# A fourth split weight block behind the inner norms, the silu table behind the root, and the last input chunk product by product, in a two-layer hybrid decoder

## What is computed

```
for l in range(DEPTH):
    ada = silu(c) @ w_ada[l] + b_ada[l]
    sh1, sc1, g1, sh2, sc2, g2 = split(ada, 6)
    u = x * (1 + sc1) + sh1
    mix = token_mixer(u, w_in[l], ...)
    x = layer_norm(ALPHA * x + (1 + g1) * mix, ln1_g[l], ln1_b[l])
    u = x * (1 + sc2) + sh2
    a, b = split(u @ w_ffn_in[l], 2)
    x = layer_norm(ALPHA * x + (1 + g2) * ((silu(a) * b) @ w_ffn_out[l]), ln2_g[l], ln2_b[l])
```

## Time and profile before

| what | value |
|---|---|
| time, median of 3 | 1686.99 us (1684.29 to 1687.72) |
| the profiled execution: its time, its span | 1685.16 us, 1683.3 us |
| instructions | 21326 |
| PE busy | 1623.5 us (96%) |
| DVE busy | 1001.8 us (60%) |
| ACT busy | 623.5 us (37%) |
| mean granted TensorE clock | 0.991 |
| DMA | 193.07 MB, mean 115 GB/s |

### The profile page before, as it was taken

One profiled execution on the slowest core, in us unless ns is written; L12 is line 12 of the kernel. 1 busy time (PEld: TensorE's weight loads), 2 busy tenths in 40 slices (PEclk: granted clock), 3 DMA queues, 4 the chain that ended last, 5 costly groups with the idle time before them and its releaser, 6 DMA issues.

```text
span 1683.3 us, 21326 instructions
## 1 busy us (share of the span) xinstructions
PE 1623.5 (96%) x8406; PEld 1277.1 (76%) x8406; DVE 1001.8 (60%) x1557; ACT 623.5 (37%) x1117; POOL 51.7 (3%) x102
## 2 busy tenths in 40 slices
PE   6999999999999999999989999999999999999997
PEld 3778677677778888888868776766777788888886
DVE  2777687758685555546567657766557533333444
ACT  3432454445253322222253325445534533222221
POOL 1000000000001001100000000000000000000000
PEclk8999999999999999999999999999999999999999
DMA  9754222134327666664427231111222233333332
GB/s 304 219 168 128 74 63 64 51 99 140 101 64 211 187 194 183 188 185 148 140 53 200 75 88 38 39 38 34 80 88 88 84 92 100 101 100 119 91 93 74
DMA packets 278450, 193.07 MB, mean 115 GB/s; under 512 B 8344, under 2 KB 264912, under 8 KB 278352
## 3 DMA queue, kind: packets, MB, share of 16 engines
q1 hardware_dynamic: 264112, 147.95, 30.4%
q0 software_dynamic: 12320, 43.11, 8.6%
q10 hardware_dynamic: 1920, 0.66, 0.2%
HBM read 189.59 MB, written 2.10 MB: 114 GB/s over the span
## 4 chain that ended last, share of the span: by engine, by line
PE 87%; DVE 7%; ACT 2%; issue 2%; DMA 1%; SPq 0%; DVEq 0%; ACTq 0%
PE banks L1587 22%; PE banks L1589 22%; PE banks L1588 22%; PE banks L1709 3%; PE banks L1740 3%; PE banks L1768 2%; DMA ada_first<-in_w_ada_dram 1%; PE banks L1629 1%; PE banks L1715 1%; PE banks L1625 1%; PE banks L1626 1%; DVE w_lo L957 1%; PE banks L1719 1%; PE banks L1644 1%; PE banks L1645 1%
## 5 line engine op out<-in xcount | busy, mean ns | idle before, releaser
L1587 PE MATMUL banks<-u_hi,w_hi 128*128 128x512 f32 x1144 | 470.5, 411 | 15.8 <-DVE w_lo L957 12.5
L957 DVE TENSOR_TENSOR w_lo<-ring,w_hi 128x1024 fp32r<-128x1024 f32 (+2 forms) x243 | 290.6, 1198 | 298.9 <-ACT w_hi L696 298.0
L1589 PE MATMUL banks<-u_hi,w_lo 128*128 128x512 f32 x1144 | 449.5, 393 | 0.0
L1588 PE MATMUL banks<-u_lo,w_hi 128*128 128x512 f32 x1144 | 449.0, 392 | 0.0
L696 ACT ACTIVATE w_hi<-ring 128x1024 fp32r<-128x1024 f32 (+2 forms) x246 | 253.8, 1032 | 198.5 <-PE banks L1589 74.5
L1587 PEld LDWEIGHTS banks<-u_hi,w_hi 128*128 128x128 f32 x1144 | 216.5, 189 | 67.9 <-DVE w_lo L957 13.2
L1589 PEld LDWEIGHTS banks<-u_hi,w_lo 128*128 128x128 f32 x1144 | 216.2, 189 | 46.5
L1588 PEld LDWEIGHTS banks<-u_lo,w_hi 128*128 128x128 f32 x1144 | 217.2, 190 | 35.8
L849 ACT ACTIVATE probs<-banks,neg_max 128x128 f32<-128x128 f32 (+3 forms) x192 | 99.2, 525 | 159.5 <-DVE neg_max L1376 159.5
L1587 PE MATMUL banks<-h_hi,w_hi 128*128 128x512 f32 x352 | 138.5, 394 | 0.0
L1589 PE MATMUL banks<-h_hi,w_lo 128*128 128x512 f32 x352 | 137.0, 389 | 0.0
(11 more groups left out here) (253 smaller groups left out, 2145.4 us busy)
## 6 DMA issues: line engine op xcount, KB each, us to landing
ring<-in_w_ffn_in_dram SPq DMA_DIRECT2D x88, 512.0 KB, 3.9
ada_ring<-in_w_ada_dram POOLq DMA_DIRECT2D x80, 512.0 KB, 4.3
ring<-in_w_in_dram SPq DMA_DIRECT2D x72, 512.0 KB, 3.8
ring<-in_w_ffn_out_dram SPq DMA_DIRECT2D x32, 448.0 KB, 3.4
ada_first<-in_w_ada_dram SPq DMA_DIRECT2D x16, 512.0 KB, 8.5
ring<-in_w_out_dram SPq DMA_DIRECT2D x16, 512.0 KB, 3.6
ring<-in_w_ffn_out_dram SPq DMA_DIRECT2D x16, 512.0 KB, 4.1
w<-in_cmp_w_k_dram SPq DMA_DIRECT2D x8, 512.0 KB, 5.6
```

The lines of the kernel that those rows point to most:

```text
L957: V.tensor_tensor(lo, src, hi.bitcast(fp32), ALU.subtract).then_inc(split_lo, 1)
L1587: M(bank, wh[:, block], sh[:, k, :], start=start, stop=False)
L1588: M(bank, wh[:, block], sl[:, k, :], start=False, stop=False)
L1589: return M(bank, wl[:, block], sh[:, k, :], start=False, stop=stop)
```

## The change

1. fb1 in both layers and kwn in layer 1 (FOURTH_SPLIT, `is_fourth`) get a split buffer of their own, `fourth_hi` and `fourth_lo`, in a part of the arena that holds other tiles at other times. ScalarE makes the high half right behind the eight inputs of the norm, without waiting for the product three blocks before; VectorE makes the low half behind the last `u_lo`. The blocks leave `prepared_at`. The slots of the others stay as they were.
2. The table load for Silu in the inner norm moves from behind the inputs to right behind the root.
3. In `project_first` the last chunk goes product by product: high and low weights against the high input, then the low input, then the next product. The wait for the low input stands behind two matmuls.

```
@@
+def is_fourth(l, name):
+    return name == FOURTH_SPLIT[0] or (name == FOURTH_SPLIT[1] and l > 0)
+FOURTH_SPLIT = ("fb1", "kwn")
@@ prepared_at
-            if nl < DEPTH and SPLIT[ni] not in FIRST_SPLIT and (nl, SPLIT[ni]) not in FIRST_LAYER_SPLIT:
+            if nl < DEPTH and SPLIT[ni] not in FIRST_SPLIT + FOURTH_SPLIT and (nl, SPLIT[ni]) not in FIRST_LAYER_SPLIT:
@@ build
+        fourth_hi = at("fourth_hi", 40, 2, fp32r)[:, :, :].rearrange("p a n -> p (a n)")
+        fourth_lo = at("fourth_lo", 42, 2, fp32r)[:, :, :].rearrange("p a n -> p (a n)")
@@ split_slot
+            if is_fourth(l, name):
+                return fourth_hi[:, 0:size], fourth_lo[:, 0:size]
@@ prepare (scalar)
-                if n >= NQ:
+                if n >= NQ and not is_fourth(l, name):
@@ layernorm (scalar)
                 nc.scalar.activation(ln_s[:, 2, :], ln_s[:, 2, :], ACT.Sqrt, bias=eps[:, :]).then_inc(std_ready, 1)
+                if which == 0:
+                    nc.scalar.activation(table_out[:, :], eps[:, :], ACT.Silu)
...
                     sub_layer_input(n + 1, m, res[:, m, :], mul_u[:, w, m:m + 1], add_u[:, w, m:m + 1])
-                if which == 0:
-                    nc.scalar.activation(table_out[:, :], eps[:, :], ACT.Silu)
+                if not last:
+                    prepare(l + which, FOURTH_SPLIT[which])
@@ project_first
                     pe.wait_ge(high, count + k + 1)
+                    if k == KD - 1:
+                        for j, (name, bank) in enumerate(zip(names, out)):
+                            wh, wl = split_slot(l, name)
+                            M(bank, wh[:, block], sh[:, k, :], start=False, stop=False)
+                            M(bank, wl[:, block], sh[:, k, :], start=False, stop=False)
+                            if j == 0:
+                                pe.wait_ge(ready, count + k + 1)
+                            done(l, name, M(bank, wh[:, block], sl[:, k, :], start=False, stop=True))
+                        break
```

More of the change, by code:

```diff
@@ L1628, in project_first @@
                     for name, bank in zip(names, out):
-                        last = M(bank, split_slot(l, name)[0][:, block], sl[:, k, :], start=False, stop=k == KD - 1)
-                        if k == KD - 1:
-                            done(l, name, last)
+                        M(bank, split_slot(l, name)[0][:, block], sl[:, k, :], start=False, stop=False)
             def tokens(l, jobs, width):
```

## The result

The median after the change is **1672.0 us** (four runs, 1671.75 to 1672.6), beside 1685.64 for the kernel before (four runs, 1681.88 to 1687.72). The ratio is 0.9922, with a 95% interval of 0.9903 to 0.9941: 13.6 us faster, against 1673.6 forecast. The profiled execution took 1672.01 us with a span of 1670.2, where the one before had 1683.3; the mean granted clock is 0.997 in place of 0.991. Some of that difference does not come from the change: from 12 to 24 us, long before the first changed place, the clock was 0.72 before and 1.00 after. No time was won by it: the changed run reached the last chunk of wo0 and wo1 0.10 us later (438.76 against 438.66).

What follows compares the result with a forecast made beforehand. TensorE, busy 96% of the span, bounds the kernel, so only its rests can be won. Gains 0.9 + 5.3 + 1.6 + 4.7 = 12.5 us give 1672.7 from the profiled execution or 1674.5 from the median; middle 1673.6, range 1671 to 1676.

Steps and rivals of the forecast that it cites:

- wo2: Two places after the last chunk of wo0 and wo1: wo0's bank frees 0.45 us earlier each, 0.9 us together.
- fb1: Both layers, after fa0, fb0, fa1: weights prepared early remove 2.73 us lost each, less 0.1 charged; gain 5.3 us.
- charge of 0.1 for the third matmul: Last chunk of fa0, fb0, fa1: waiting earlier for `u_lo` costs 0.1 us, bounds 0 and 0.9.
- The clock behind fb1: Layer 0, ten matmuls behind fb1's rest: without the rest no clock fall, 1.6 us gained; ends 0 and 1.6.
- The Silu table: Inner norm: the load behind the root fits ScalarE's wait, 1.49 us into 1.74; cost 0, margin 0.25 us.
- kwn: Start of layer 1: kwn starts on its slot, but VectorE's chain limits the gain to 4.7 us; ends 2 and 5.4.
- The sum: Whole kernel: 0.9 + 5.3 + 1.6 + 4.7 = 12.5 us gained.
- (a): Clock still falls in layer 0's ffn or behind the token products' new rest; 1.6 to 4 us not won; chance 0.15.
- (b): Margins of 0.1 us at fb1 and the third matmul fail by up to half a microsecond; 1675 us; chance 0.1.
- (c): Table load holds ScalarE behind the root beyond 1.74 us, costing 1.24 at two norms; 1676 us; chance 0.05.
- (d): Fourth blocks are ready, but fb1's bank and vsg0 hold TensorE as long; gain 2 us, 1684; chance 0.03.
- (e): Layer 1's token products, with new rests, keep TensorE at 1.2 GHz; slower, 40 us of it gives 1692; chance 0.03.

Runs made afterwards that it cites:

- the run shown above: The changed kernel run again unaltered on another chip, as yardstick for later runs: 1671.96 us, ratio 0.9928 to the kernel before.

## Why the prediction was right, step by step

The forecast was 1673.6 us, the measurement 1672.0, inside the forecast's own range. The signs that it named are all there.

- **wo2.** 0.45 us per place was forecast by two pitches; layer 0 shows 0.48. The experiment with the old order puts the wait back (1.5 us against 0.6).
- **fb1.** Forecast 2.63 per layer, with a charge of 0.1 for the third matmul. Measured 2.71 in layer 0, and 3.26 together with wo2 in layer 1. The charge was not needed: the third matmul's weight load waited 0.11 us, the matmul itself did not. The margin was larger on the chip: `fourth_lo` was ready 0.30 us before fb1's start, where the forecast has 0.15 between the same two points, because `fourth_hi` begins 0.60 us ahead of the last chunk, where the table load in its place began 0.49 ahead. In these rows an activation starts a little before the row of the one ahead of it ends (495.80 against 495.90), and the load did not. The old order on its own shows the second condition that the prediction named, fa0's bank.
- **The clock behind fb1.** 1.6 us was forecast, 1.71 measured between the two profiles. Of this 0.15 is not the clock: in layer 1 of the kernel before, at the upper level, the ten matmuls behind the rest took 2.42 us, and without a rest they take 2.27. So the clock's own part is the 1.56 that the forecast used. As a price per execution it holds for this pair only: the other profile of the kernel before lost it in both layers, and there it is 1.6 us more from fb1 in layer 1 to the end (361.9 against 360.3). How often it is lost in the executions without a profile is not shown, so that one loss was the right number to forecast is partly luck. This fits the wider spread of the kernel before (1681.88 to 1687.72, against 1670.28 to 1673.27 in all runs of the changed one), but much of the spread arises ahead of the change: in the ten profiles the last chunk of wo0 and wo1 in layer 0 starts between 436.99 and 440.74 us. From that start to the span's end it is 1231.44 and 1231.38 us in the two profiles of the changed kernel, and 1244.64 and 1246.04 in the two of the kernel before. So the gain is 13.2 to 14.7 us in these profiles, depending on how often the clock fell.
- **The Silu table.** Cost 0 with a margin of 0.25 was forecast; 0.23 us of ScalarE's wait is left. ScalarE's load starts 0.02 us behind the end of the root, takes 1.28 us as before, and the next activation follows it at once. The Trainium skill's page "ScalarE: Activation LUTs", section What ACT_TABLE_LOAD costs, puts a switch at about 2.66 us, a drain included. By an estimate from that figure and the small activation's 0.20 us, the first `u_hi` would have been late by 1.1 us; the prediction left the 0.20 out and has 0.9. The trace does not agree in this place, as no drain is to be seen in it. Put in front of fb1, the load costs 2.7 us in two layers.
- **kwn.** The rest of 5.37 us went, and 4.84 of it reached vsg2; forecast was 4.7. Most of the 0.14 between them has the cause of fb1's margin: `fourth_hi` begins 0.61 us ahead of the last chunk (868.87 against 869.48), the forecast has 0.49. A slip in its sum, 876.24 + 0.69 = 876.95 where it is 876.93, changes nothing. The step that decided it, that VectorE's chain and not TensorE sets this stage, was shown by the run with fb1's buffer alone (4.1 us, not 7; 3.99 by the starts) and by the one that moves VectorE's work (4.6 us gained, at an unchanged amount of work). The new rest before vsg0 was forecast as 2.0 and measured as 1.82.
- **The sum.** 12.5 was forecast, and 13.1 is the difference of the spans. Of the missing 0.6 the table above has 0.25 at the four places of wo2 and fb1 (0.48 + 2.71 + 3.26 against 6.2), 0.14 at kwn, 0.11 in fb1's first ten matmuls and 0.1 in small shifts elsewhere. The forecast of 1673.6 was 1.6 too high for a second reason, some 0.9 of it: it took the middle between the profiled execution and the median shown, and the profiled execution (1685.16) was nearer to the middle of all later runs of the kernel before (1684.8 to 1685.64).
- **The rivals.** (a), a fall of the clock behind the new rest, did happen in one of the two profiles of the changed kernel, and cost nothing. What the prediction allowed for, that it is partly hidden under VectorE's chain, was true of all of it. (b), (c) and (d) show no sign; (e) would need a clock that stays low through the token products, and the fall there was over before vsg1. The row that spoke for it, 0.72 from 12 to 24 us, does not belong to its place either: the changed kernel's profile has 1.00 there.

## What to carry to other kernels

A product that waits for prepared weights behind a norm can be given a buffer of its own and be prepared in the first free moment of the engine that prepares; look then at what is next in line (here the bank of the first product, and the copies and additions on VectorE), since the gain is cut to that. Put a table load into a wait that exists anyway, and measure that wait first. When one rest is removed and a new one appears on the same engine's waits, the next change is named: here it was the order of VectorE's work, worth another 4.6 us.

## What was not expected of the hardware

The fall of the clock after a rest is not the same from run to run. In the two profiles of the kernel before, three of four rests of 2.57 us before fb1 were followed by a fall; of nine rests of 1.6 to 1.8 us before fb1 and vsg0 in the changed kernel and the experiments, one was (the run shown above); all four rests of 4.3 to 5.2 us, before kwn, were. And in these runs a fall cost time only where TensorE sets the stage: behind kwn and before vsg0 it cost nothing that can be measured (25.05 us with the deeper fall, 25.09 with the lesser; 21.12 with one, 21.10 without), behind fb1 it cost 1.6 us.
